# Hybrid attention/convolution encoder layer on one core: TensorE's side matmuls in the middle of their dense tile, and loads and orders changed beside it

## Chip, cores and metric

One core of one Trainium2 chip runs the whole program. The metric is the device time of an execution in microseconds; lower is better. Three executions of the kernel before took 2691.98, 2694.58 and 2695.61 us.

## What is computed

One layer of an encoder, applied to two batches with shared weights: a prompt of 512 tokens and a sample of 2048 tokens, 2560 in all, model width 1024. Inputs and outputs are float32.

```python
h = _rms(x, norm1_g)
proj = h @ w_in                       # 1024 -> 512 q, 128 k, 128 v, 1024 GLU input
q, k = per-head RMSNorm(q), per-head RMSNorm(k)      # 8 query heads, 2 key heads, 64 wide
attn = _window_attention(q, k, v, attn_sink)         # 128-query blocks against 384 keys, ALiBi, sink
u = a * sigmoid(gate); u = depthwise_conv31(u); u = silu(layernorm(u))
x = x + concatenate([attn, u]) @ w_out
h2 = _rms(x, norm2_g)
g = silu(depthwise_conv3(h2 @ ffn_w_gate))           # 1024 -> 2816
x = x + (g * (h2 @ ffn_w_up)) @ ffn_w_down
```

## The kernel before, in words

**Dense work in slots.** Activations lie transposed (features on the 128 partitions, tokens along the row). Each weight tile of 128 outputs is split into a high and a low part (`weights`, float32r), and each activation too (`h_hi`/`h_lo`, `cat_hi`/`cat_lo`, `hw_hi`/`hw_lo`, `mid`); a product is hi*hi + hi*lo + lo*hi. One **slot** is one dense tile: 8 input tiles of 128 times 3 products, 24 matmuls into one bank of PSUM. There are 374 slots (`SLOT`), in phases: A (14 slots for each of 5 chunks of 512 tokens: the input projection, 128x512 results), O (8 slots per chunk: the output projection), and F (66 slots for each of 4 windows of 438 tokens: G, gate and up tiles by turns, then D, down tiles). The order is A0 A1 A2 A3, the first 6 slots of A4, O0, the rest of A4, then F0 with O1 in its middle, F1 with O2, F2 with O3, F3 with O4. The last two windows (406 tokens each) follow in another scheme, 198 block products ("pair" code, from L2250 on), which has no side work.

**Every engine walks the same list of slots.** In its iteration n, ScalarE (ACT) and VectorE (DVE) first handle the result of slot n-1 (`before`): they wait for the counter `s_used` that the last matmul of that tile raises, and evict or post-process it: for a gate tile ACT copies it (`gb`, L1369), DVE applies three taps (`cv`, L1788, L1791, L1794); for an up tile DVE multiplies it in (L1801), ACT and DVE split the product (L1386, L1807). Then they split the weights of slot n+2 (ACT L1144, DVE L1558), then do the side work that the planner's lists `ACT_SIDE[n]` and `DVE_SIDE[n]` name, and DVE ends with a share of the depthwise convolution (`cc`, L1661/L1665), shared out by the room that a planner (`conv_room`) sees in each slot. All queues are strictly in order. So iteration n of ACT and DVE runs beside the dense tile n of TensorE.

**TensorE's side work.** `PE_SIDE[n]` names the small matmuls of slot n: `scores` (6 matmuls, L2208), `transpose` of probabilities (4 per tile, L2219), `values` (8 or 12, L2230), `qk_sum` (L2173), `qk_spread` (L2194), `v_transpose` (L2181), `norm1` (L2156), the LayerNorm and RMSNorm sums (L2238, L2243, L2248). In the kernel before they are issued behind the 24 matmuls of tile n and ahead of tile n+1, each behind its own waits. For attention block N (20 blocks of 128 queries, first slots and steps in `ATTN_AT`) the lists are:

```python
for _t in range(GROUP):                      # GROUP = 4
    PE_SIDE[_b + _t].append(("scores", _N, _t))
    DVE_SIDE[_b + _t + 1].append(("bias", _N, _t))
...
PE_SIDE[_b + 7 + _i // 2].append(("transpose", _N, _g, _k))
ACT_SIDE[_b + 8 + _i // 2].append(("copy_t", _N, _g, _k))
PE_SIDE[_b + 10].append(("values", _N))
```

`scores(N, t)` with t > 0 waits until DVE's `bias(N, t-1)` (L1726, two operations, then small ones) has read the two score banks; that `bias` stands in `DVE_SIDE[b + t]`, the same slot number as the waiting scores. `transpose` number i waits for ACT's copy (`copy_t`, L1289) of transpose i-3; `values` waits for the last copy. `qk_spread(c, m)` waits for DVE's `qk_norm(c, m-1)` (L1629), `norm1` for `token_inverse` (L1565), the sums for DVE's additions of the same slot.

**Loads.** SyncE (SP) issues nearly all loads, in order: in iteration n the weights of slot n+4 (once tile n is done), then what the slot's conditions name. `load_cat(c, half)` loads one half of the output projection's input, a high and a low part: half 0 are the attention rows, half 1 the convolution rows; they were stored from GpSimd's (POOL's) queue (`store_attn`, `store_ln`). Before, half 1 is issued in iteration START["O", c] - 4, half 0 in START["O", c] - 3, and the 8 residual loads in START["O", c] - 1. The first matmul of an O phase waits for all four.

**Start.** The first chunk's norm is applied after the projection: ACT squares `x0` (L1168), DVE adds the squares (L1586, L1589), and TensorE sums them over the partitions (`first_sum`, L2162) behind tile 1. The weights of slots 0 to 3 are split before the loop.

Of the kernel before, what the change touches and what calls it, by code (L numbers as in the profile page):

```python
# [26 lines left out]
KT = D_MODEL // P  # L27
# [60 lines left out]
SLOT = []  # L88
START = {}
# [9 lines left out]
SLOTS = len(SLOT)  # L99
# [75 lines left out]
for _c in range(CHUNKS):  # L175
    _b = AT_SLOT["A", _c, 0]
    if _c + 1 < CHUNKS:
        for _f, _t in ((2, 0), (4, 2)):
            ACT_SIDE[_b + _f] += [("token_squares", _c + 1, _t), ("token_squares", _c + 1, _t + 1)]
        ACT_SIDE[_b + 5].append(("token_root", _c + 1))  # L180
        DVE_SIDE[_b + 5].append(("token_inverse", _c + 1))
        PE_SIDE[_b + 5].append(("norm1", _c + 1))
        ACT_SIDE[_b + 6].append(("scale_copy", _c + 1))
        for _p, _f in enumerate((7, 8, 10, 11)):
            DVE_SIDE[_b + _f].append(("norm_h", _c + 1, _p))
            ACT_SIDE[_b + _f].append(("h_high", _c + 1, _p))
            DVE_SIDE[_b + _f + 1].append(("h_low", _c + 1, _p))
    PE_SIDE[_b + 1 + NORMED].append(("qk_sum", _c))
    PE_SIDE[_b + 7].append(("v_transpose", _c))
    ACT_SIDE[_b + 7].append(("qk_root", _c))  # L190
    ACT_SIDE[_b + 8].append(("v_out", _c))
    DVE_SIDE[_b + 8].append(("qk_inverse", _c))
    ACT_SIDE[_b + 9].append(("qk_high", _c))
    DVE_SIDE[_b + 9].append(("qk_low", _c))
    POOL_SIDE[_b + 9].append(("v_store", _c))
    for _m in range(NORMED):
        PE_SIDE[_b + 10 + _m].append(("qk_spread", _c, _m))
        DVE_SIDE[_b + 11 + _m].append(("qk_norm", _c, _m))
        POOL_SIDE[_b + 12 + _m].append(("qk_store", _c, _m))

for _c in range(CHUNKS):
# [284 lines left out]
def encoder_layer(nc, x, x_tok, w_in, w_out, w_ffn, w_down, w_pass, params, consts, y):  # L486
    with ExitStack() as ctx:
# [305 lines left out]
        def _(sp):  # L793
# [135 lines left out]
            for p in range(1, PIECES):  # L929
                load_first(p)  # L930
            load_weight(1)
            sp.dma_start(pick[:], consts[:, C_PICK:C_SPREAD]).then_inc(s_const, 16)
            sp.dma_start(ident[:], consts[:, P:2 * P]).then_inc(s_const, 16)
            sp.dma_start(spread_raw[:], consts[:, C_SPREAD:C_BIAS]).then_inc(s_const, 16)
            sp.dma_start(bias[:], consts[:, C_BIAS:C_SLOPE]).then_inc(s_const, 16)
            sp.dma_start(slope[:], consts[:, C_SLOPE:C_COLS]).then_inc(s_const, 16)
            load_weight(2)
            load_weight(3)
            u_v = u_d.rearrange("j p n -> p j n")
            edges = (0, PROMPT_U - HALO, PROMPT_U, U_COLS - HALO)  # L940
# [15 lines left out]
            for n in range(SLOTS):  # L956
                s = SLOT[n]
                if n + RING < SLOTS:
                    load_weight(n + RING)
                if EDGES_AT <= n < EDGES_AT + len(edges):  # L960
                    store_edge(n - EDGES_AT)
                if PADS_AT <= n < PADS_AT + len(pads):
                    store_pad(n - PADS_AT)
                if s[0] == "A" and s[1] + 1 < CHUNKS:
                    c, f = s[1] + 1, s[2]
                    if f == 0:
                        load_xt(c, 0)
                        load_xt(c, 1)
                        load_xs(c, 0)
                        load_xs(c, 1)  # L970
                    if f == 2:
                        load_xt(c, 2)
                        load_xt(c, 3)
                    if f in (8, 9):
                        load_xs(c, f - 6)
                if n == START["F", 0, 0] - 4:
                    for p in range(PIECES):
                        load_window(0, p)
                if s[0] == "D" and s[2] == 1 and s[1] + 1 < PLAIN and 1 <= s[3] < 1 + PIECES:
                    load_window(s[1] + 1, s[3] - 1)  # L980
                if s[0] == "G" and s[2] == 0 and s[4] == 1 and 1 <= s[3] < 1 + KT:
                    load_y(s[1], s[3] - 1)
                for c in range(CHUNKS):
                    if n == START["O", c] - 4:
                        load_cat(c, 1)
                    if n == START["O", c] - 3:
                        load_cat(c, 0)
                    if n + 1 == START["O", c]:
                        load_residual(c)
                if n in PAIR_LOADS:  # L990
                    load_pair_window(0, PAIR_LOADS[n])
                if n == LAST + GU_TILES:
                    for a in ("A21", "A22", "A11", "A12"):
                        load_part(0, a)
# [142 lines left out]
        def _(act):  # L1137
# [320 lines left out]
            for p in range(1, PIECES):  # L1458
                first_high(p)
            weight_high(1)  # L1460
            weight_high(2)
            for p in range(PIECES):
                first_squares(p)
            weight_high(3)
            act.wait_ge(s_const, 16 * 5)
            nc.scalar.activation(spread[:], spread_raw[:], ACT.Copy).then_inc(s_sprd, 1)
# [88 lines left out]
        def _(dve):  # L1555
# [367 lines left out]
            for p in range(1, PIECES):  # L1923
                first_low(p)
            weight_low(1)
            weight_low(2)
            for p in range(1, PIECES):
                first_add(p)
            weight_low(3)
            dve.wait_ge(s_const, 16 * 5)  # L1930
            nc.vector.tensor_scalar(qg[:], slope[:, 0:AT], col("q_g"), None, ALU.mult).then_inc(s_set, 1)
# [103 lines left out]
        def _(pe):  # L2035
# [34 lines left out]
            def project(n, c, f):  # L2070
                e = OUTPUT["A", c, f]
                bank_free(e)
                weight_ready(n)
                out = bank[out_bank(e)]
                hi, lo, a, b = h_hi[c % 2], h_lo[c % 2], whi[n % RING], wlo[n % RING]
                for k in range(KT):
                    if f == 0 and k % PK == 0:
                        pe.wait_ge(s_hlo, PIECES * c + k // PK + 1)
                    for i, (l, r) in enumerate(((a, hi), (a, lo), (b, hi))):
                        mm = nc.tensor.matmul(out[:], l[:, k, :], r[:, k, :],  # L2080
                                              start=(k == 0 and i == 0), stop=(k == KT - 1 and i == 2))
                mm.then_inc(s_used, 1)
# [21 lines left out]
            def out_project(n, c, o):  # L2104
                e = OUTPUT["O", c, o]
                bank_free(e)
                weight_ready(n)
                if o == 0:
                    pe.wait_ge(s_cat, 64 * (c + 1))
                out = bank[out_bank(e)]  # L2110
                a, b = whi[n % RING], wlo[n % RING]
                for k in range(KT):
                    for i, (l, r) in enumerate(((a, cat_hi), (a, cat_lo), (b, cat_hi))):
                        mm = nc.tensor.matmul(out[:], l[:, k, :], r[:, k, :],  # L2114
                                              start=(k == 0 and i == 0), stop=(k == KT - 1 and i == 2))
                mm.then_inc(s_used, 1)

            def gate_up(n, w, h, i, s):
                e = OUTPUT["G", w, h, i, s]
                bank_free(e)  # L2120
                weight_ready(n)
                if h == 0 and i == 0 and s == 0:
                    pe.wait_ge(s_hwlo, PIECES * (w + 1))
                a, b = whi[n % RING], wlo[n % RING]
                out = bank[out_bank(e)][:, 0:TC if s else TH]
                for k in range(KT):
                    for j, (l, r) in enumerate(((a, hw_hi), (a, hw_lo), (b, hw_hi))):
                        mm = nc.tensor.matmul(out, l[:, k, :], r[:, k, 1:TC + 1] if s else r[:, k, :],  # L2128
                                              start=(k == 0 and j == 0), stop=(k == KT - 1 and j == 2))
                mm.then_inc(s_used, 1)  # L2130

            def down(n, w, h, i):
                weight_ready(n)
                a, b = whi[n % RING], wlo[n % RING]
                for q in range(KT):
                    o, k = divmod(KT * i + q, FH)
                    e = OUTPUT["D", w, h, o]
                    out = bank[out_bank(e)][:, 0:TC]
# [157 lines left out]
                        mm.then_inc(s_dn, 1)  # L2296
                mm.then_inc(s_used, 1)

            pe.wait_ge(s_set, 4)
            for n in range(SLOTS):  # L2300
                s = SLOT[n]
                if s[0] == "A":
                    c, f = s[1], s[2]
                    if n == 0:
                        first_project()
                    else:
                        project(n, c, f)
                    if n == 1:
                        first_sum()
                        pe.wait_ge(s_const, 16 * 5)  # L2310
                elif s[0] == "O":
                    out_project(n, s[1], s[2])
                elif s[0] == "G":
                    gate_up(n, *s[1:])
                else:
                    down(n, *s[1:])
                for t in PE_SIDE[n]:
                    if t[0] == "norm1":
                        spread_scale(t[1])
# [14 lines left out]
                    elif t[0] == "ln_var":  # L2334
                        ln_var(t[1])
                    elif t[0] == "norm2":
                        norm2_sum(t[1])
            pe.wait_ge(s_y, 2 * KT * PLAIN - 3)
            for k in range(PRODS):
                if PROD[k][0] == "P":  # L2340
# [84 lines left out]
```

## Time and profile before

| | us |
|---|---|
| three executions | 2691.98, 2694.58, 2695.61; median 2694.58 |
| the profiled execution | 2696.35, its span 2694.5 |
| TensorE matmul busy | 2645.7 (98% of the span) |
| TensorE weight load busy | 2346.5 (87%) |
| VectorE busy | 1822.0 (68%) |
| ScalarE busy | 1259.0 (47%) |
| GpSimd busy | 193.6 (7%) |
| mean granted TensorE clock | 0.995 |

The span is from the first to the last instruction of the profiled execution; 1.85 us of its time lie around the span. A matmul's end is modelled, and matmuls overlap in the pipeline, so "98% busy" is not 98% of the peak; the distance between the starts of two matmuls says how fast they go.

### The profile page before, as it was taken

How to read it: one execution, taken by the hardware profiler on the slowest of the kernel's cores; microseconds unless marked ns; L12 is line 12 of the kernel's file. 1: busy time of each engine (PE TensorE's matmuls, PEld its weight loads, DVE VectorE, ACT ScalarE, POOL GpSimd, SP SyncE). 2: the span in 40 equal slices, each digit the busy share in tenths (PEclk: the TensorE clock that was granted, in tenths of full speed). 3: DMA queues.
4: the chain of work that ended last, by engine and by line, in shares of the span. 5: the costliest groups of instructions: out<-in, count | busy, mean ns of one | idle time of the engine just before them, and what ended most of it. 6: DMA issues, size and time to landing. Idle time of an engine off the chain costs nothing.

```text
span 2694.5 us, 35290 instructions
## 1 busy us (share of the span) xinstructions
PE 2645.7 (98%) x13216; PEld 2346.5 (87%) x13216; DVE 1822.0 (68%) x3020; ACT 1259.0 (47%) x2031; POOL 193.6 (7%) x332
## 2 busy tenths in 40 slices
PE   8999999999999999999999999999999999999998
PEld 6777777788888998888998888998889999999998
DVE  4665747798676876576877577877256576766764
ACT  5354564466535447336446336447134333433432
POOL 0110021100010000110000110000010000000001
PEclk9999999999999999999999999999999999999999
DMA  8867769734753443753443753443754522221211
GB/s 319 319 215 250 255 239 364 269 124 130 269 184 118 150 133 112 295 182 114 153 134 114 278 179 125 149 134 125 270 174 159 182 76 62 71 63 59 67 55 66
DMA packets 138761, 453.74 MB, mean 168 GB/s; under 512 B 24448, under 2 KB 37120, under 8 KB 121952
## 3 DMA queue, kind: packets, MB, share of 16 engines
q1 hardware_dynamic: 111616, 349.17, 38.4%
q0 software_dynamic: 26976, 102.32, 10.5%
q8 instruction: 106, 1.74, 0.3%
q14 instruction: 63, 0.52, 0.1%
HBM read 362.63 MB, written 88.79 MB: 168 GB/s over the span
## 4 chain that ended last, share of the span: by engine, by line
PE 90%; DMA 3%; DVE 3%; ACT 2%; issue 2%; SPq 0%; POOL 0%; DVEq 0%; ACTq 0%; POOLq 0%
PE bank L2128 31%; PE bank L2144 14%; PE bank L2276 12%; PE bank L2080 10%; PE bank L2114 8%; PE bank L2292 7%; PE bank L2230 2%; PE bank L2208 2%; PE bank L2219 2%; DMA cat_lo<-cat_scratch 2%; DMA xt<-x_tok 1%; DMA wraw<-w_in_t 0%; PE bank L2194 0%; PE bank L2173 0%; DVE xs L1573 0%
## 5 line engine op out<-in xcount | busy, mean ns | idle before, releaser
L2128 PE MATMUL bank<-hw_hi,weights 128*128 128x440 f32 (+1 forms) x2816 | 812.3, 365 | 0.0
L2128 PEld LDWEIGHTS bank<-hw_hi,weights 128*128 128x128 f32 x2816 | 530.0, 188 | 47.9 <-issue 12.9
L2128 PE MATMUL bank<-hw_lo,weights 128*128 128x440 f32 (+1 forms) x1408 | 510.8, 363 | 0.0
L2144 PE MATMUL bank<-mid,weights 128*128 128x438 f32 x2112 | 431.9, 364 | 0.0
L2144 PEld LDWEIGHTS bank<-mid,weights 128*128 128x128 f32 x2112 | 396.0, 189 | 33.3 <-issue 6.8
L1558 DVE TENSOR_TENSOR weights<-wraw,weights 128x1024 fp32r<-128x1024 f32 x286 | 348.8, 1220 | 106.0 <-ACT weights L1144 105.3
L1665 DVE SCALAR_TENSOR_TENSOR cc<-win,par,cc 128x512 f32<-128x512 f32 x600 | 414.3, 743 | 0.0
L1144 ACT ACTIVATE weights<-wraw 128x1024 fp32r<-128x1024 f32 x286 | 301.7, 1055 | 236.2 <-DMA wraw<-w_down_t 157.1
L2080 PE MATMUL bank<-h_hi,weights 128*128 128x512 f32 x1104 | 360.2, 400 | 0.0
L2128 PEld LDWEIGHTS bank<-hw_lo,weights 128*128 128x128 f32 x1408 | 264.4, 188 | 16.6 <-issue 1.0
L2080 PEld LDWEIGHTS bank<-h_hi,weights 128*128 128x128 f32 x1104 | 209.2, 189 | 53.5 <-issue 5.7
L2080 PE MATMUL bank<-h_lo,weights 128*128 128x512 f32 x552 | 218.2, 395 | 0.0
L2114 PE MATMUL bank<-cat_hi,weights 128*128 128x512 f32 x640 | 204.9, 396 | 10.7 <-DMA cat_lo<-cat_scratch 10.7
L1401 ACT ACTIVATE part_hi<-part_raw 128x512 fp32r<-128x512 f32 x198 | 119.8, 623 | 152.5 <-DMA part_raw<-w_pass_t 88.6
L2292 PE MATMUL bank<-mid,part_hi 128*128 128x406 f32 x704 | 188.2, 348 | 2.3 <-DVE mid L1899 1.9
L1843 DVE TENSOR_TENSOR part_lo<-part_raw,part_hi 128x512 fp32r<-128x512 f32 x198 | 134.7, 687 | 65.7 <-ACT part_hi L1401 63.7
L2114 PEld LDWEIGHTS bank<-cat_hi,weights 128*128 128x128 f32 x640 | 121.7, 190 | 39.8 <-issue 14.4
L1369 ACT ACTIVATE gb<-bank 128x440 f32<-128x440 f32 x88 | 47.2, 536 | 221.8 <-PE bank L2128 217.1
L1788 DVE TENSOR_SCALAR cv<-gb,par 128x438 f32<-128x438 f32 x88 | 44.8, 509 | 147.7 <-ACT gb L1369 147.5
L2292 PEld LDWEIGHTS bank<-mid,part_hi 128*128 128x128 f32 x704 | 131.1, 189 | 4.3 <-DVE mid L1899 4.0
L2114 PE MATMUL bank<-cat_lo,weights 128*128 128x512 f32 x320 | 125.9, 394 | 0.0
L2080 PEld LDWEIGHTS bank<-h_lo,weights 128*128 128x128 f32 x552 | 104.6, 190 | 23.5 <-issue 0.8
(215 smaller groups left out, 3724.3 us busy)
## 6 DMA issues: line engine op xcount, KB each, us to landing
weights<-weight_scratch SPq DMA_DIRECT2D x88, 1024.0 KB, 5.6
wraw<-w_ffn_t SPq DMA_DIRECT2D x176, 512.0 KB, 3.5
wraw<-w_down_t SPq DMA_DIRECT2D x88, 512.0 KB, 3.5
weight_scratch<-weights POOLq DMA_DIRECT2D x22, 1024.0 KB, 7.7
part_raw<-w_ffn_t SPq DMA_DIRECT2D x88, 256.0 KB, 2.7
part_raw<-w_pass_t SPq DMA_DIRECT2D x44, 256.0 KB, 2.6
cat_hi<-cat_scratch SPq DMA_DIRECT2D x10, 1024.0 KB, 7.2
cat_lo<-cat_scratch SPq DMA_DIRECT2D x10, 1024.0 KB, 10.2
```

What stands on the lines that cost most here:

```text
L1144: nc.scalar.activation(whi[n % RING], wraw[n % RING][:], ACT.Copy).then_inc(s_whi, 1)
L1401: nc.scalar.activation(p_hi[k % HI_RING][:], p_raw[part_of(k)][:], ACT.Copy).then_inc(s_whi, 1)
L1558: nc.vector.tensor_tensor(wlo[n % RING], wraw[n % RING][:], whi[n % RING].bitcast(F32), ALU.subtract) \
L1665: nc.vector.scalar_tensor_tensor(acc, win[i][:, tap:tap + TB], w_tap, acc, ALU.mult, ALU.add).then_inc(s_cv, 1)
L1843: nc.vector.tensor_tensor(p_lo[part_of(k)][:], p_raw[part_of(k)][:], p_hi[k % HI_RING][:].bitcast(F32), ALU.subtract).then_inc(s_wlo, 1)
L2080: mm = nc.tensor.matmul(out[:], l[:, k, :], r[:, k, :], start=(k == 0 and i == 0), stop=(k == KT - 1 and i == 2))
L2114: mm = nc.tensor.matmul(out[:], l[:, k, :], r[:, k, :], start=(k == 0 and i == 0), stop=(k == KT - 1 and i == 2))
L2128: mm = nc.tensor.matmul(out, l[:, k, :], r[:, k, 1:TC + 1] if s else r[:, k, :], start=(k == 0 and j == 0), stop=(k == KT - 1 and j == 2))
L2144: mm = nc.tensor.matmul(out, l[:, q, :], mid[:, k, part, :], start=(k == 0 and j == 0), stop=(k == FH - 1 and j == 2))
L2208: mm = nc.tensor.matmul(bank[SCORE[g]][:, P * ks[0]:P * (ks[-1] + 1)], q[rows, t, :], k[rows, P * (n + ks[0]):P * (n + ks[-1] + 1)], start ...
L2276: mm = nc.tensor.matmul(out, l[:, t, :], r[:, t, cols], start=(p in (1, 2, 5) and t == 0 and j == 0), stop=(t == KH - 1 and j == 2), skip_ ...
L2292: mm = nc.tensor.matmul(bank[BANK_Y[n % 4]][:, 0:TP], l[:, (deep * o + t) % KH, :], mid2[:, t, part, i, :], start=(t == 0 and z == 0), sto ...
```

## The change

Of the kernel's text it moves these things; nothing is computed that was not computed before.

1. The side work of slot n is issued by a new helper `side_work(n)`, called inside the loop of `project`, `out_project`, `gate_up` and `down` behind the 12th of the 24 matmuls (k or q == 4 of 8). Slot 0, whose tile is `first_project`, keeps it behind. `first_sum` stays behind tile 1.
2. `h_high` (ACT's split of the next chunk's input) goes one slot later; DVE's `h_low` stays, so that both are in the same slot.
3. `qk_norm` goes to the head of its slot's list on DVE.
4. At the start the load of the weights of slot 2 goes ahead of the five loads of constants; ACT's squares and DVE's additions go ahead of the split of those weights.
5. For chunks 1 to 4 half 0 of `cat` is loaded in iteration START["O", c] - 6 instead of - 3, now ahead of half 1.

```diff
@@ -183,7 +183,7 @@
         for _p, _f in enumerate((7, 8, 10, 11)):
             DVE_SIDE[_b + _f].append(("norm_h", _c + 1, _p))
-            ACT_SIDE[_b + _f].append(("h_high", _c + 1, _p))
+            ACT_SIDE[_b + _f + 1].append(("h_high", _c + 1, _p))
             DVE_SIDE[_b + _f + 1].append(("h_low", _c + 1, _p))
@@ -195,7 +195,7 @@
     for _m in range(NORMED):
         PE_SIDE[_b + 10 + _m].append(("qk_spread", _c, _m))
-        DVE_SIDE[_b + 11 + _m].append(("qk_norm", _c, _m))
+        DVE_SIDE[_b + 11 + _m].insert(0, ("qk_norm", _c, _m))
         POOL_SIDE[_b + 12 + _m].append(("qk_store", _c, _m))
@@ -929,12 +929,12 @@
             load_weight(1)
+            load_weight(2)
             sp.dma_start(pick[:], consts[:, C_PICK:C_SPREAD]).then_inc(s_const, 16)
...
             sp.dma_start(slope[:], consts[:, C_SLOPE:C_COLS]).then_inc(s_const, 16)
-            load_weight(2)
             load_weight(3)
@@ -983,7 +983,7 @@
                     if n == START["O", c] - 4:
                         load_cat(c, 1)
-                    if n == START["O", c] - 3:
+                    if n == START["O", c] - (6 if c else 3):
                         load_cat(c, 0)
@@ -1458,9 +1458,9 @@
             weight_high(1)
-            weight_high(2)
             for p in range(PIECES):
                 first_squares(p)
+            weight_high(2)
             weight_high(3)
@@ -1923,9 +1923,9 @@
             weight_low(1)
-            weight_low(2)
             for p in range(1, PIECES):
                 first_add(p)
+            weight_low(2)
             weight_low(3)
@@ -2074,6 +2074,8 @@
                 for k in range(KT):
+                    if k == KT // 2:
+                        side_work(n)
                     if f == 0 and k % PK == 0:
                         pe.wait_ge(s_hlo, PIECES * c + k // PK + 1)
...
@@ -2296,24 +2304,8 @@
+            def side_work(n):
+
                 for t in PE_SIDE[n]:
                     if t[0] == "norm1":
                         spread_scale(t[1])
...
+            pe.wait_ge(s_set, 4)
+            for n in range(SLOTS):
...
+                else:
+                    down(n, *s[1:])
+                if n == 0:
+                    side_work(n)
```

The same two lines (`side_work(n)` at k or q == KT // 2) stand in `out_project`, `gate_up` and `down`.

## Rows read from the trace of the kernel before

**Rows 1.** The page: the span, and TensorE's busy time.
```profile
span 2694.5 us, 35290 instructions
PE 2645.7 (98%) x13216; PEld 2346.5 (87%) x13216; DVE 1822.0 (68%) x3020; ACT 1259.0 (47%) x2031; POOL 193.6 (7%) x332
```

**Rows 2.** What TensorE waited for, whole run: us in total, times, longest.
```profile
PE bank L2114 <- DMA cat_lo<-cat_scratch: 10.7, 4, 3.4
PE bank L2194 <- DVE qk L1629: 5.4, 3, 4.5
PE bank L2162 <- DVE x_acc L1589: 4.7, 1, 4.7
PE bank L2208 <- DVE row_max L1726: 2.6, 4, 1.1
```

**Rows 3.** The chain of waits, G tiles of slots 272 to 275: start, us, what.
```profile
1619.52 0.73 PE bank L2208 x6
1620.24 5.01 PE bank L2128 x24
1625.25 0.72 PE bank L2208 x5
```

**Rows 4.** The timeline of VectorE beside rows 3: start, us, line and operation.
```profile
1620.13 0.51 DVE L1788 TENSOR_SCALAR cv<-gb,par 128x438 f32<-128x438 f32 x1
1621.97 1.22 DVE L1558 TENSOR_TENSOR weights<-wraw,weights 128x1024 fp32r<-128x1024 f32 x1
...
1623.59 0.55 DVE L1726 CUSTOM_DVE_ANT_0 S<-bank,bias 128x384 f32<-128x384 f32 x1
...
1628.67 0.55 DVE L1726 CUSTOM_DVE_ANT_0 S<-bank,bias 128x384 f32<-128x384 f32 x1
```

**Rows 5.** The chain of waits between D tiles of slots 292 and 293.
```profile
1719.15 0.72 PE bank L2208 x6
```

**Rows 6.** The timeline of VectorE beside rows 5.
```profile
1721.83 0.55 DVE L1726 CUSTOM_DVE_ANT_0 S<-bank,bias 128x384 f32<-128x384 f32 x1
```

**Rows 7.** The chain of waits, transposes behind the G tile of slot 279.
```profile
1651.13 0.87 PE bank L2219 x8
```

**Rows 8.** The timeline of ScalarE beside rows 7.
```profile
1654.26 1.06 ACT L1289 ACTIVATE S<-bank 128x512 f32<-128x512 f32 x2
```

**Rows 9.** The chain of waits, A tiles: slots 16 and 17, then 70 and 71.
```profile
127.13 0.55 PE bank L2208 x6
...
484.51 5.80 PE bank L2080 x24
...
498.66 0.79 PE bank L2208 x6
```

**Rows 10.** The timeline of VectorE in the first of these two stretches.
```profile
128.19 0.42 DVE L1726 CUSTOM_DVE_ANT_0 S<-bank,bias 128x256 f32<-128x256 f32 x1
```

**Rows 11.** Groups by line: xcount, then busy us and mean ns of one.
```profile
L2208 PE MATMUL bank<-kw_hi,qt_hi 64*128 64x384 f32 x128 | 28.4, 440 | 0.8 <-DVE row_max L1726 0.8
...
L2219 PE MATMUL bank<-ident,S 128*128 128x128 f32 x448 | 58.2, 272 | 0.2 <-ACT S L1289 0.2
```

**Rows 12.** The chain of waits: the last `cat` load of chunk 1.
```profile
712.90 11.40 DMA cat_lo<-cat_scratch
```

**Rows 13.** Stretches: us, then per engine busy us (instructions), granted clock, DMA share, GB/s.
```profile
26.90:35.20 8.30, 8.30 (x27) 6.20 (x26) 2.65 (x5) 6.40 (x9) 0.60 (x2) 0.70 1.01 366
...
711.00:724.00 13.00, 11.52 (x62) 10.60 (x60) 8.51 (x14) 4.95 (x10) 0.00 (x0) 1.00 1.01 427
724.00:732.00 8.00, 7.57 (x28) 6.11 (x29) 1.14 (x3) 0.00 (x0) 0.00 (x0) 0.79 1.02 411
1117.00:1128.00 11.00, 9.17 (x46) 8.30 (x44) 5.36 (x11) 4.16 (x8) 0.00 (x0) 1.00 1.01 425
```

**Rows 14.** The timeline of the start: ScalarE's third weight split, VectorE's last addition.
```profile
18.10 1.06 ACT L1144 ACTIVATE weights<-wraw 128x1024 fp32r<-128x1024 f32 x1 [4.71 <-DMA wraw<-w_in_t]
...
25.00 0.69 DVE L1589 TENSOR_TENSOR x_acc<-x_acc 128x512 f32<-128x512 f32 x1
```

More of the change, by code:

```diff
@@ L2112, in out_project @@
                 for k in range(KT):
+                    if k == KT // 2:
+                        side_work(n)
                     for i, (l, r) in enumerate(((a, cat_hi), (a, cat_lo), (b, cat_hi))):
@@ L2126, in gate_up @@
                 for k in range(KT):
+                    if k == KT // 2:
+                        side_work(n)
                     for j, (l, r) in enumerate(((a, hw_hi), (a, hw_lo), (b, hw_hi))):
@@ L2135, in down @@
                 for q in range(KT):
+                    if q == KT // 2:
+                        side_work(n)
                     o, k = divmod(KT * i + q, FH)
@@ L2297, in pair_down @@
                 mm.then_inc(s_used, 1)
[L2299 to L2316, printed above, removed]
+            def side_work(n):
                 for t in PE_SIDE[n]:
@@ L2337, in _ @@
                         norm2_sum(t[1])
+            pe.wait_ge(s_set, 4)
+            for n in range(SLOTS):
+                s = SLOT[n]
+                if s[0] == "A":
+                    c, f = s[1], s[2]
+                    if n == 0:
+                        first_project()
+                    else:
+                        project(n, c, f)
+                    if n == 1:
+                        first_sum()
+                        pe.wait_ge(s_const, 16 * 5)
+                elif s[0] == "O":
+                    out_project(n, s[1], s[2])
+                elif s[0] == "G":
+                    gate_up(n, *s[1:])
+                else:
+                    down(n, *s[1:])
+                if n == 0:
+                    side_work(n)
             pe.wait_ge(s_y, 2 * KT * PLAIN - 3)
```

## The prediction, made before the changed kernel was built or run

> **What bounds the kernel now.** I read the page first: TensorE's matmuls are busy for 2645.7 of 2694.5 us [rows 1]. Little can be gained by waiting less, and whatever makes TensorE wait costs its full time. Then what TensorE waited for: four items that the change touches, 10.7 us for the load of `cat`, 5.4 for `qk_norm`, 4.7 for the first sum of squares and 2.6 for `bias` [rows 2]. That is 23.4 us, the most that the removal of waits alone can give. Third, the chain of waits beside VectorE's timeline in one stretch [rows 3, 4]: it shows how much room the side work has where it stands. Tile 273 (gate) ends at 1619.52, its scores take 0.73, tile 274 runs from 1620.24 to 1625.25, and only then come the next scores. From the end of tile 273 VectorE does three taps, the weight split and the two `bias` operations, back to back, the last until 1623.59 + 0.55 = 1624.14. The scores behind tile 274 want that `bias`, and find it ready 1.1 us before they start. So the whole side chain is hidden, by about a microsecond, behind a full dense tile. The change takes half of that tile away.
>
> **Part 1, side work in mid-tile.** It adds and removes no matmul. TensorE's stream stays in order, so the second half of the tile is queued behind a side matmul that waits, and with it the end of the tile, `s_used`, the evictions of ACT and DVE, and SP's load of the weights of slot n+4. What was hidden behind 24 matmuls must now be ready after 12. Since iteration n of VectorE begins at the end of tile n-1, the price of a wait is: (producer's end minus end of tile n-1) minus half a tile. A plain G tile takes 4.8 us (24 starts 0.20 apart; 5.01 with the turn back from the scores [rows 3]), so the half is 2.4; an A tile takes 5.5, half 2.75.
>
> - Scores with t > 0, 60 of them (20 blocks, 3 each): 24 fall in G slots, 18 in D, 17 in A and 1 in O, by the planner's list. The number of blocks shows in the 128 + 32 first-product matmuls of scores, two for each of 80 scores; rows 11 has the 128. In G after a gate tile: 1624.14 - 1619.52 = 4.62, less 2.40, is 2.2 us late. After an up tile: 1628.67 + 0.55 = 1629.22, minus 1625.25, is 3.97; 1.6 late [rows 3, 4]. With a mean of 1.9, 24 cost **45 us**. The bounds are 1.2 (if ACT's swish, which lags in this stretch, comes up to date) and 2.4.
> - D: the tile ends at 1719.15, `bias` at 1721.83 + 0.55 = 1722.38 [rows 5, 6]: 3.23 less 2.40 is 0.8 late; 18 cost **15**.
> - A and O, 18: in slot 17 the tile before ends at 127.13 and `bias` at 128.19 + 0.42 = 128.61 [rows 9, 10]: 1.5 us against 2.75, nothing. In slot 71 the tile before ends at 484.51 + 5.80 = 490.31, and the scores start at 498.66 [rows 9]: 8.3 less 2.75 is 5.6 late, of which some was waited for already. The ends are 0 and 5; I take 1.0, since most A slots look like the first: **18**.
> - Transposes in G: behind tile 279, which ends at 1651.13, ACT's first copy ends at about 1654.26 + 0.53 = 1654.79 [rows 7, 8]: 3.66 less 2.40 is 1.3 late. 448 transposes make 112 groups [rows 11], two to a tile; 29 of these tiles are G, of which a third (the first of a block) waits for nothing near, and the third of a block comes off with less. 19 at 0.8: **15**. The 8 like ones in A, with a longer ACT list, at 1.5: **12**. `values` in G, 10 at 0.3: **3**.
> - `norm1` (4), the sums over partitions and the first `qk_spread` of a chunk wait for work of their own slot number too. I have no row for each; bounded by 0 and by half a tile (2.75) for some 12 of them, I take **10**.
>
> The sum is 118 us. The turn into side work and back costs 0.2 us per side tile in either place [rows 3]; I take no difference, with bounds of -10 and +10 us for 174 side tiles.
>
> **Part 2 and 3, `h_high` and `qk_norm`.** `h_high` a slot later frees ACT from waiting for `norm_h`; DVE's `h_low` then waits in its stead, behind it the convolution, in the same slot. No time of its own: `h` of the next chunk is due two slots later, and that is its cover; gone, it would cost 1 us or so per chunk. `qk_norm` first in its list can remove up to 5.4 us [rows 2], but the longest of these waits (4.5) lies in the first chunk, where VectorE is late with all it has, and now the spread asks for it half a tile sooner. I take **-2**.
>
> **Part 4, start.** ACT's third weight split starts at 18.10 after a wait of 4.71 for its load, and the squares stand behind it; DVE's last addition is at 25.00 [rows 14]. With squares first they start at about 13.4 and the sum is there before tile 1 ends at 21: the 4.7 us go [rows 2], and with them the fall of the clock that follows, 8.3 us at 0.70 [rows 13], which cost 8.3 * 0.30 = 2.5. Together **-7**. Late next are the weights of slot 2, at about 20.8, as TensorE comes free for them.
>
> **Part 5, `cat`.** Its last load starts at 712.90, when the DMA engines are full (share 1.01, 427 GB/s), and lands 11.40 us later [rows 12, 13]. Two of the four loads, issued three slots (some 15 us) sooner, find the engines free. On SP they pass two weight loads, which are two tiles ahead of need, and wait for attention stores that are issued four slots before, on POOL's queue. All 10.7 us go [rows 2], and two falls of the clock, 8.0 us at 0.79 each [rows 13], or 1.7 each: **-14**. Late next is the convolution half, one slot earlier than the old last half.
>
> **Sum.** 118 - 2 - 7 - 14 = +95. The profiled execution took 2696.35 (span 2694.5 and 1.85 around it), 1.8 above the median; on the median 2694.6 that is 2789.6, say **2789 us**.
>
> **Rivals.**
>
> *The lists of ACT and DVE catch up (half the stalls).* Both engines are idle for a third of the span or more [rows 1]; each stall of TensorE gives them time to work off what they carry over, above all in the A phases. Against it: in rows 4 the chain starts at the tile's end itself. With half of 118 the sum is +36: 2731.
>
> *The clock oscillates.* TensorE's granted clock was at 2.4 GHz while it waited before 1128 (1.00), and fell to 1.2 GHz for a part of the 8 us after 724 (mean 0.79) [rows 13]. Both followed waits of about 3 us; so the new waits, 1 to 5 us each and in some 95 tiles, are near what tips it. If half of them did at 1.7 each, that adds 80: 2870. Against: most of mine are under 2.3 us. The Trainium skill (TensorE: Matmul & The Clock Gate, "A second HAM failure mode: psum-queue depth-cycling") says that frequent short idles between groups of matmuls make the clock swing between its two levels; by that rule this case would be the likelier one. No row here has such a series of short waits, so none bears it out.
>
> *Faster.* If the bias chain does not begin at the end of the tile but was carried over from the iteration before, its end moves forward with the stall, TensorE soon waits for nothing, and the 23 us of parts 2 to 5 are left: 2672. The point is a mean stall under 0.25 us in these 95 tiles; place: VectorE's taps and weight split ahead of `bias`. Against it: the first tap needs the finished gate tile (1620.13, just after 1619.52 [rows 3, 4]), and 3.4 us of operations follow until the second `bias` starts.
>
> *No change:* stalls and gains cancel at about 23 us of stalls; a coincidence.
>
> **How the numbers follow.** Forecast 0.62, lists catch up 0.19, clock 0.12, faster 0.04, no change 0.03. The range goes from 2731 to 2860: the low end is the second case, the high end takes the upper bounds in G and A (24 * 2.4 and 18 * 3 add 48, turns 10) and part of the clock case. No measurement of this kernel can tell less than about 0.2% (5.4 us) from no change. Faster: 0.04; same 0.03; slower 0.93.
>
> **What would show it.** In the profile after: TensorE waits for `row_max` (L1726) some 50 times, 60 to 80 us in all, in place of 4 times and 2.6; waits for ACT's copies (L1289) some 20 times; tiles in G with scores 7.5 us apart in place of 5.7; `cat` and `x_acc` gone from the list of waits; granted clock near 0.99. I am wrong if the scores' waits sum to under 25 us, or if the clock's mean is below 0.97.

## The result, and the profile after

The kernel after takes 2832.04 us (median of 4 executions, 2828.76 to 2838.28); the kernel before, on the same chip, 2693.28. The ratio is 1.0517, with a 95% interval of 1.0497 to 1.0538: 139 us slower. Forecast were 2789 us, with a range of 2731 to 2860. The profiled execution took 2832.09, its span is 2830.3.

The page of the kernel after, for [rows 1]: the span is 135.8 us longer, the count of matmuls is the same, and yet TensorE is busy for 39 us more.

```profile
span 2830.3 us, 35290 instructions
PE 2684.7 (95%) x13216; PEld 2368.6 (84%) x13216; DVE 1819.5 (64%) x3020; ACT 1255.9 (44%) x2031; POOL 193.4 (7%) x332
```

What TensorE of the kernel after waited for, for [rows 2] (us in total, times, longest):

```profile
PE bank L2216 <- DVE row_max L1726: 56.3, 32, 5.6
PE bank L2238 <- ACT S L1289: 12.4, 10, 4.2
PE bank L2227 <- ACT S L1289: 10.3, 7, 3.1
PE bank L2251 <- DVE ln_acc L1690: 10.2, 4, 3.3
PE bank L2246 <- DVE ln_acc L1675: 9.5, 4, 3.5
PE bank L2102 <- ACT weights L1144: 8.2, 1, 8.2
PE bank L2164 <- DVE t_rs L1565: 6.5, 3, 4.5
PE bank L2216 <- DVE qt_lo L1714: 6.2, 4, 2.2
PE bank L2202 <- DVE qk L1629: 4.4, 4, 2.2
```

`cat` and `x_acc`, 15.4 us in [rows 2], are gone. In their stead stand the scores (L2216) behind `bias`, `values` (L2238) and transposes (L2227) behind ACT's copies, the two LayerNorm sums (L2251, L2246) and `norm1` (L2164). The 8.2 us for the first weights (L2102) were there before, with 8.1. All lines of this view add up to 135.1 us; before it was 39.2. So 96 of the 136 us are new idle time.

The same stretch as in [rows 3], in the chain of waits of the kernel after (start, us, what): the second half of gate tile 273 ends at 1731.05, and tile 274 begins.

```profile
1728.44 2.61 PE bank L2134 x12
...
1731.07 0.55 ACT gb L1369
...
1732.90 0.68 DVE cv L1794
1733.57 1.14 DVE weights L1558
1734.71 0.47 DVE S L1726
1735.17 0.01 DVE row_max L1726
1735.18 0.47 DVE S L1726
...
1735.72 0.79 PE bank L2216 x4
1736.51 3.86 PE bank L2134 x12
```

From the end of the tile the chain goes through ACT's copy, three taps, the weight split and two `bias` operations, and back into TensorE 4.67 us later. TensorE itself has only 12 matmuls to do meanwhile. Its timeline gives what was idle there and one tile earlier (in brackets):

```profile
1727.65 0.45 PE L2216 MATMUL bank<-kw_hi,qt_hi 64*128 64x384 f32 x2 [0.98 <-DVE row_max L1726]
...
1735.72 0.44 PE L2216 MATMUL bank<-kw_hi,qt_hi 64*128 64x384 f32 x2 [2.27 <-DVE row_max L1726]
```

The last line of the chain shows the other loss. The 12 matmuls behind the wait take 3.86 us, the 12 before it 2.61. The windows view of these stretches (us, busy us by engine, granted clock, DMA share, GB/s) says why: the clock was full until 1736 and at 0.67 behind it.

```profile
1727.00:1736.00 9.00, 6.08 (x34) 5.20 (x34) 5.96 (x18) 4.88 (x8) 0.00 (x0) 1.00 0.32 116
1736.00:1740.30 4.30, 4.30 (x19) 3.72 (x18) 0.21 (x2) 1.99 (x3) 0.00 (x0) 0.67 0.00 0
```

Over the whole span the mean granted clock is 0.982 (before 0.995). As an estimate, a mean clock c over a span costs (1 - c) * span: 51 us after, 13 before, 38 more. With 96 us of idle time that makes 134 of the 136 us. I call these two sums "waits" and "clock" below.

### The profile page after: what moved, and what is told of

The parts are those of the page before. It is cut to its first block, busy times and chain, and to the rows that moved or that the text cites. A ratio compares the mean times of both kernels' runs of the same rounds, so it can differ in the third digit from the quotient of the medians.

```text
span 2830.3 us, 35290 instructions
## 1 busy us (share of the span) xinstructions
PE 2684.7 (95%) x13216; PEld 2368.6 (84%) x13216; DVE 1819.5 (64%) x3020; ACT 1255.9 (44%) x2031; POOL 193.4 (7%) x332
## 4 chain that ended last, share of the span: by engine, by line
PE 75%; DVE 10%; ACT 5%; DMA 5%; issue 4%; SPq 0%; POOL 0%; DVEq 0%; ACTq 0%; POOLq 0%
PE bank L2134 24%; PE bank L2284 11%; PE bank L2152 11%; PE bank L2082 8%; PE bank L2118 7%; PE bank L2300 7%; DVE weights L1558 2%; PE bank L2238 2%; PE bank L2216 2%; PE bank L2227 2%; DMA wraw<-w_down_t 1%; DMA xt<-x_tok 1%; DVE S L1726 1%; ACT weights L1144 1%; DVE cc L1665 1%
## 5 line engine op out<-in xcount | busy, mean ns | idle before, releaser
L2134 PE MATMUL bank<-hw_hi,weights 128*128 128x440 f32 (+1 forms) x2816 | 824.0, 369 | 0.0
L2134 PEld LDWEIGHTS bank<-hw_hi,weights 128*128 128x128 f32 x2816 | 539.1, 191 | 52.3 <-issue 16.2
L2134 PE MATMUL bank<-hw_lo,weights 128*128 128x440 f32 (+1 forms) x1408 | 516.9, 367 | 0.0
L1801 DVE TENSOR_TENSOR cv<-bank,cv 128x438 f32<-128x438 f32 x88 | 54.0, 613 | 127.9 <-PE bank L2134 103.7
```

## The experiments

Theory: all the loss comes from the missing distance between a producer and the place of its side work, directly as waits and through them as falls of the clock. Rivals: the turn from dense to side matmuls inside an accumulation costs time; the moved orders (`h_high`, `qk_norm`) cost time; the scores only stand in front of another wait.

| kernel | us | ratio, 95% interval | waits | clock (mean) |
|---|---|---|---|---|
| before | 2693 to 2696 | 1 | 39 | 13 (0.995) |
| after | 2832.0 | 1.0517 (1.0497 to 1.0538) | 135 | 51 (0.982) |
| e1 middle alone | 2869.1 | 1.0647 (1.0621 to 1.0673) | 157 | 57 (0.980) |
| e2 parts 2 to 5 alone | 2669.2 | 0.9906 (0.9889 to 0.9922) | 20 | 8 (0.997) |
| e3 behind 18 of 24 | 2730.6 | 1.0142 (1.0122 to 1.0163) | 69 | 16 (0.994) |
| e10 behind 6 of 24 | 2995.0 | 1.1116 (1.1095 to 1.1137) | 249 | 102 (0.966) |
| e4 scores behind the tile | 2752.0 | 1.0214 (1.0190 to 1.0239) | 71 | 25 (0.991) |
| e5 bias a slot earlier | 2755.3 | 1.0228 (1.0202 to 1.0254) | 79 | 28 (0.990) |
| e6 parts 4 and 5 alone | 2676.3 | 0.9939 (0.9924 to 0.9953) | 30 | 11 (0.996) |
| e7 filler | 2826.5 | 1.0501 (1.0483 to 1.0519) | 102 | 34 (0.988) |
| e8 weight split behind bias | 2796.5 | 1.0382 (1.0365 to 1.0399) | 113 | 28 (0.990) |
| e9 all a slot apart | 2686.8 | 0.9965 (0.9951 to 0.9979) | 33 | 8 (0.997) |
| e11 e9, queries and norm too | 2673.6 | 0.9919 (0.9904 to 0.9934) | 24 | 5 (0.998) |
| e12 the kernel of e2 again | 2670.3 | 0.9908 (0.9891 to 0.9924) | 21 | 5 (0.998) |

Waits are the sum of all lines of the view of TensorE's waits, clock is (1 - c) * span with c to three places (so within 1.5 us), both of the profiled execution, in us. That execution is not always a typical one: in e1 and e4 it is 8 and 6 us faster than the median of the second column, in e6 6 us slower.

### e1 and e2: the two halves of the change

e1 is the kernel after with parts 2 to 5 undone. e2 has parts 2 to 5 and this in TensorE's list:

```diff
                 for k in range(KT):
-                    if k == KT // 2:
-                        side_work(n)
...
-                if n == 0:
-                    side_work(n)
+                side_work(n)
```

> Part 1 alone, parts 2 to 5 undone. My theory: the middle of the tile carries the whole loss and the other parts gain about 20 us, so this is the slowest of all, 2832 + 20 = 2852 us, with cat and the first sum of squares back among TensorE's waits. Rival (h_high a slot later and qk_norm ahead cost time too): at or below 2832.

> Parts 2 to 5 alone, the side work behind the tile as before. My theory: 2693 less the 23 us of waits and clock falls, 2672, half-clock time down from 30 us to some 10. Rival (the waits only move to the next thing that is late): 2685 to 2695. Rival (orders cost): above 2695.

The middle alone costs 174 us (2869.1), parts 2 to 5 alone gain 25 (2669.2, forecast 23), and e2 is the fastest kernel of the study. The whole loss lies in part 1; the rival of the costly orders falls. e1 is also the cleanest measure of part 1's waits: 157 us against 39 before are 118 us more, which is the sum forecast for them. The halves do not add up quite: on top of the middle, parts 2 to 5 gain 37, not 25. In e1 `qk_norm` stands among the waits with nearly three times what it has in the kernel after:

```profile
PE bank L2118 <- DMA cat_lo<-cat_scratch: 12.2, 4, 3.9
PE bank L2202 <- DVE qk L1629: 11.9, 8, 4.3
```

In e2 what the parts aimed at is all but gone. The largest wait that is left is the one for the first weights, and next one for the weights of slot 5 (L2080, at 41.67 us): their load started at 21.94 and took 17.25. Slot 2, which the prediction named as late next, started at 21.00 without a wait.

```profile
PE bank L2100 <- ACT weights L1144: 7.6, 1, 7.6
PE bank L2080 <- DVE weights L1558: 3.4, 1, 3.4
...
PE bank L2208 <- DVE row_max L1726: 1.8, 3, 1.1
...
PE bank L2194 <- DVE qk L1629: 0.7, 2, 0.5
```

### e3 and e10: how far into the tile

```diff
-                    if k == KT // 2:
+                    if k == KT - 2:          # e3; in e10: k == 2
                         side_work(n)
```

> The whole change, but the side work behind the 18th matmul of 24. If the loss is what is missing between the producer and half a tile, each wait shrinks by 1.2 us (G, D) or 1.4 (A): of the 56 us of waits for row_max some 15 are left, the clock falls a few times only, 2715 us. If the loss is the turn from dense to side matmuls and back inside an accumulation, nothing changes: 2830.

> The whole change, with the side work behind the 6th matmul of 24. Behind the tile 2669, after 18 matmuls 2731, after 12 2832: the waits are now late by another 1.2 us each, in some 90 tiles, so idle time of 135 us becomes about 235, and with more waits over 3 us half-clock time rises from 105 to some 180 us (38 us lost): 2965. If the lists of ACT and DVE catch up once TensorE waits this much, it levels off: 2880.

Behind 24, 18, 12 and 6 of the 24 matmuls the time is 2669, 2731, 2832 and 2995 us: each quarter costs more than the one before, 61, 101 and 163. The turn into side work and back is the same in the last three, so it is not what costs. The waits for `bias` in e3, and in e10:

```profile
PE bank L2216 <- DVE row_max L1726: 24.0, 16, 4.2
```

```profile
PE bank L2216 <- DVE row_max L1726: 103.7, 43, 7.0
```

With 56.3 us and 32 times between them: each wait grows by the matmuls taken away, more waits turn up, and the clock takes its share (16, 51, 102 us). The timelines of TensorE show it tile by tile. Ahead of the scores in an up tile (behind a gate tile; 11 of them) it stands idle for 1.08 us in e3, 2.28 in the kernel after and 3.48 in e10, in the median: 1.20 more each time, which is what six matmuls 0.20 apart take. Ahead of those in a gate tile (behind an up tile; 13 of them) it is 0, 0.98 and 2.19.

Both expectations were too low, by 16 and 30 us. For e3 I had expected some 15 us of waits for `bias` and 24.0 were left. For e10 the waits came to 249 us instead of 235, since the scores in D tiles, which waited for 2.5 us in all in the kernel after, waited for 14, and the clock lost 51 us more instead of 38. The engines' lists did not catch up.

### e4: the scores stay behind the tile

`side_work` runs twice, in the middle for all but `scores`, behind the tile for `scores`:

```diff
+def IN_MIDDLE(t):
+    return t[0] != "scores"
...
                 for t in PE_SIDE[n]:
+                    if IN_MIDDLE(t) != middle:
+                        continue
```

> The whole change, but the scores stay behind the tile; all other side work is in its middle. If scores are the bulk, as I forecast (78 of 118 us), waits for row_max (56 us) go but for a few, and with them about half of the clock falls: 2755. If the other side work sets the loss and the scores' waits only stood in front of it: above 2800.

2752.0 against an expectation of 2755. Scores carry 80 us of the 163 that lie between e2 and the kernel after, the rest of the side work the other 83, the clock included in both. I had given the scores 78 of 118, and the rest 40, without the clock. In waits alone it is 64 for the scores (135 to 71) and 51 for the rest (71 to 20).

### e5 and e8: change the chain ahead of the scores

e5: `bias` a slot earlier, possible since the scores are now done in mid-tile. e8: in slots with a `bias`, DVE's weight split goes behind it.

```diff
-        DVE_SIDE[_b + _t + 1].append(("bias", _N, _t))
+        DVE_SIDE[_b + _t].append(("bias", _N, _t))
```

```diff
-                if RING <= n + AHEAD < SLOTS and SPLIT[n + AHEAD]:
+                later = any(t[0] == "bias" for t in DVE_SIDE[n])
+                if RING <= n + AHEAD < SLOTS and SPLIT[n + AHEAD] and not later:
                     weight_low(n + AHEAD)
...
+                if RING <= n + AHEAD < SLOTS and SPLIT[n + AHEAD] and later:
+                    weight_low(n + AHEAD)
```

> The whole change, and bias one slot earlier on DVE's list: since scores(N, t) are now done in the middle of tile b + t, bias(N, t) can stand in DVE_SIDE[b + t] and be ready about when that tile ends, half a tile ahead of the next scores. My theory (too little distance between producer and place): the waits for row_max fall from 56 us to under 10, half of the clock falls go, 2755 us, as with the scores behind the tile. If the loss lay in the engines being out of room as such, about 2830.

> The whole change, and in slots with a bias on DVE's list the weight split (1.22 us) stands behind it instead of ahead. If the waits are the chain that I added up from the end of the tile before, each wait of scores in G and D tiles shrinks by up to 1.2 us: row_max 56 us becomes some 30, 2795. If the bias was held by the scores themselves or by ACT: no change, 2830.

e5 takes 2755.3 us, as expected, and as much as e4: giving the scores distance is worth the same whether the scores go back or the `bias` comes forward. In its list of waits `row_max` does not stand at all; ACT's copies, the LayerNorm sums and `norm1` lead as before. e8 takes 2796.5 (expected 2795). Its waits for `bias`:

```profile
PE bank L2219 <- DVE row_max L1726: 39.8, 33, 5.6
```

About the same number of waits, 16.5 us less, and 23 us less of clock: one operation of 1.22 us taken out of the chain is worth 36 us. Where the split simply stood in the chain, in the up tiles, the idle time fell from 2.28 to 1.14 us. In the gate tiles it fell from 0.98 to 0.59 only, since behind an up tile VectorE now stands idle for 0.64 us until ScalarE has its half of the product (`mid`, L1386) ready; the split had covered that wait. In the A tiles, where some slots load split weights, the waits fell from 17.9 to 15.5 us.

### e7: fill the waits instead of removing them

In the 24 gate and up tiles with scores of t > 0, two matmuls of zero weights go onto the open bank ahead of the side work. They add zero to the result.

```diff
                     if k == KT // 2:
+                        if any(t[0] == "scores" and t[2] > 0 for t in PE_SIDE[n]):
+                            for _ in range(2):
+                                nc.tensor.matmul(bank[out_bank(e)][0:CT * HALO, 0:TC if s else TH], zeros[:],
+                                                 (hw_hi[:, 0, 1:TC + 1] if s else hw_hi[:, 0, :]).bitcast(F32),
+                                                 start=False, stop=False)
                         side_work(n)
```

> The whole change, and in the 24 gate and up tiles with scores of t > 0, ahead of the side work, two matmuls of zero weights onto the open bank (they add nothing; some 1.5 us of TensorE time where it waited 2.2 on average). If the falls of the clock cost time of their own beside the idle time, the eight of them in these tiles (some 41 us at half clock, 20 us lost) go for the most part, while the filled waits cost nothing: 2815. If the clock follows the program anyway or its fall costs nothing: 2832 or more.

The groups by line show the added work, 96 records for 48 matmuls, 40 us:

```profile
L2134 PE MATMUL bank<-hw_hi,zeros 128*60 128x440 f32 x52 | 21.9, 544 | 0.0
L2134 PE MATMUL bank<-hw_hi,zeros 128*60 128x438 f32 x44 | 18.5, 543 | 0.0
```

Waits fell by 33 us and the clock's share by 17; 33 + 17 - 40 is 10, and the profiled span is 9 us shorter than that of the kernel after. The medians are 5.5 us apart, with intervals that overlap, so by time alone this run does not decide whether there is a gain. What it shows is that 40 us of extra matmuls cost nothing: 33 went into waits that were there, and the clock, whose mean over all four executions is 0.986 against 0.982, paid for the rest. The expected gain of 17 us (2815) was too high; the fillers, 1.7 us in each tile, were longer than the 1.0 us that TensorE waited in most gate tiles. That the idle time itself brings the clock down is supported by this run and by the counts of the last section; no run changed the one without the other.

### e9, e11 and e12: distance for everything

```diff
-        PE_SIDE[_b + 5].append(("norm1", _c + 1))
+        PE_SIDE[_b + 6].append(("norm1", _c + 1))
-        DVE_SIDE[_b + 11 + _m].insert(0, ("qk_norm", _c, _m))
+        DVE_SIDE[_b + 10 + _m].append(("qk_norm", _c, _m))
-    PE_SIDE[_l + LN_SUM[_c]].append(("ln_sum", _c))
+    PE_SIDE[_l + LN_SUM[_c] + (1 if _c else 0)].append(("ln_sum", _c))
-    PE_SIDE[_l + _at[5]].append(("ln_var", _c))
+    PE_SIDE[_l + _at[5] + 1].append(("ln_var", _c))
-        DVE_SIDE[_b + _t + 1].append(("bias", _N, _t))
+        DVE_SIDE[_b + _t].append(("bias", _N, _t))
-        ACT_SIDE[_b + 8 + _i // 2].append(("copy_t", _N, _g, _k))
+        ACT_SIDE[_b + 7 + _i // 2].append(("copy_t", _N, _g, _k))
```

e11 adds the same for what e9 still waited for: `load_q`, `attn_q_high`, `attn_q_low` a slot earlier (and `load_kv`, `k_high`, `k_low` for chunks 1 to 4), and the RMSNorm sum a slot later on TensorE. e12 is e2's kernel again, beside e11 on one chip.

> The whole change, with every producer and its side work put a slot further apart: bias, the copies of the transposes and qk_norm one slot earlier on DVE's and ACT's lists, norm1, the four later LayerNorm sums and all variance sums one slot later on TensorE's. If the middle of the tile costs nothing in itself and only the distance counts, nearly all new waits go (135 us of idle to 30 or so) and the clock stays up: 2680, close to the 2669 of the side work behind the tile with its lists as they are. If it costs a turn of its own, or DVE and ACT now wait for TensorE in place of the reverse and are late with the evictions: 2720 or more.

> e9 and the rest of its new waits: the keys and queries of a block are loaded and split a slot sooner, and the RMSNorm sum stands a slot later on TensorE. If the middle of the tile only needs distance, idle time falls from 33 us to some 22, and the time to 2673, as with the side work behind the tile. If something else of 10 to 15 us hangs on the middle: 2685, as e9.

> The kernel of e2 once more, beside e11 on one chip, for the comparison of the two: 2669 us again, if e2's time was no chance.

With side work in the middle of every tile e9 takes 2686.8 us and e11 2673.6: the loss of 163 us against e2 has shrunk to 3. e9's largest new wait, before e11 took it away, was:

```profile
PE bank L2216 <- DVE qt_lo L1714: 7.5, 4, 2.2
```

So the middle of the tile costs next to nothing in itself, and it gives nothing either. e12 took 2670.3 us, 3.3 less than e11; all its executions (2669.1 to 2671.3) are below all of e11 (2672.5 to 2674.5), and e11's profile has 3 us more of waits, so the difference is probably real and lies in waits that are left. Scores in neighbouring G tiles follow each other 5.73 us apart in e11 and 5.75 in e2 (medians), so leaving an open tile and coming back costs no more than the same work behind it. e2 stays the version to keep, 0.9% faster than before and the simpler one.

## Why the prediction was right, and what was off

**Direction and mechanism: right.** The price of a wait, (producer's end minus end of the tile before) minus half a tile, was forecast from [rows 3, 4] as 2.2 us behind a gate tile and 1.6 behind an up tile. In the same tiles of the kernel after it is 2.27 (tile 274) and 0.68 (tile 275), and over all G tiles 2.28 and 0.98 in the median. The second is under its lower bound of 1.2, for the reason given there: ACT's swish (L1375), which ended 0.3 us after the up tile 274 before, now ends 3.3 us ahead of that tile's end, at 1737.06. e3, e10 and e8 move the two sides of that difference one at a time, and the idle time in the up tiles follows by 1.1 to 1.2 us a step.

**The sum of waits: right in total, wrong in parts.** Forecast: 118 us added, 23 removed, 95 net. Of the 23, some 6 are falls of the clock, so in waits alone the forecast is 101 net. Measured: 39.2 to 135.1, that is 96 net; part 1 alone adds 118 (e1). The parts are less good (idle time ahead of the scores with t > 0, from TensorE's timeline, and lines of the list above, in us):

| | forecast | kernel after |
|---|---|---|
| scores in G | 45 | 36 |
| scores in D | 15 | 2.5 |
| scores in A and O | 18 | 18 |
| transposes | 27 | 10.3 |
| `values` | 3 | 12.4 |
| `norm1` and the sums | 10 | 10.2 + 9.5 + 6.5 = 26 |
| a block's first scores, behind the split of its queries (`qt_lo`) | none | 6.2 |

Three things were wrong in the reading. In D the chain of [rows 6] does not begin with the end of the tile: its weight split follows convolution operations without a gap, and in the kernel after it starts before the tile's end, so that the scores of slot 293 waited for 0.05 us instead of 0.8. In A the mean of 1.0 us was 11 waits of nothing and 7 of 1.3 to 5.6. And the item for `norm1` and the sums, for which I had no rows, had a bound of half a tile (2.75 us) that does not hold, with single waits of 4.5, 3.5 and 3.3 us. The signs said some 50 waits for `row_max` with 60 to 80 us, and there are 32 with 56; tiles in G with scores 7.5 us apart, and they are 8.3 apart in the mean. That the parts made up for one another is luck.

**The clock: the step that failed.** The sum holds nothing for new falls of the clock; they stood there as a rival with a chance of 0.12 (half of some 95 waits bring one, at 1.7 us each: 80 us, 2870). The profile shows 38 us more lost to it, in 16 more falls (22 stretches at 1.2 GHz against 6 before, by the trace's clock records), nearly all of the 43 us by which 2789 was too low. The result lies between the forecast and that rival. The argument against it, "most of mine are under 2.3 us", was too weak a one: waits of that length are where it begins (counted in the last section). The rule of the Trainium skill (TensorE: Matmul & The Clock Gate, "A second HAM failure mode: psum-queue depth-cycling"), that frequent short idles between groups of matmuls make the clock swing, pointed the right way, and this trace agrees in part: the clock did swing, but the falls went with the length of the single gap (10 of 10 over 3 us, 3 of 41 under 2 us).

**Catch-up: wrong case, as rated.** With TensorE waiting more, ACT's and DVE's lists did not recover: from e3 to e10 the waits grew from 69 to 249 us, and in the up tiles the idle time is the same 2.28 us in 8 of 11. Only the swish did.

**Parts 2 to 5: right.** Forecast -23, measured -25 (e2). Parts 4 and 5 gain 18 (e6, forecast 21), the orders 7 (forecast 2). What is missing from the 21 is at the start: TensorE begins slot 4 8.2 us sooner in e2 than before (32.55 against 40.71), but then waits 3.4 us for the weights of slot 5, so that slot 5 begins 4.6 us sooner (41.67 against 46.28), where 7 were forecast.

> Parts 4 and 5 alone (start and cat loads), all orders and the side work as before. By my terms 21 us of the 25 that parts 2 to 5 gained: 2673. If the orders (h_high, qk_norm) carry half of it: 2682.

e6 took 2676.3. `qk_norm`'s wait is back in it, which is what the orders had taken away:

```profile
PE bank L2194 <- DVE qk L1629: 6.7, 4, 4.5
```

I had expected the first chunk's wait of 4.5 us to stay whatever stands first on DVE's list; with the side work behind the tile it goes.

## What to carry to other kernels

Where side work sits in an in-order stream is a due time: before moving it up, take for each item the end of its producer relative to the event that starts the producer's chain, and compare that with what the engine has left to do until the new place. Moving the work by half a tile cost 163 us here, and moving the producers (or the place) by one slot gave back all but 3, so move both sides together or neither. Check first that the chain does begin with that event: in D tiles it did not, and the forecast there was six times too high. And price a wait of TensorE with the clock that it may take along: here that added some 40% to the idle time.

## What the runs showed of the hardware

Whether TensorE's clock fell went with how long it had just stood idle. Counted over the starts and modelled ends of all matmuls against the clock records, this many gaps were followed by a fall (within 5 us of their end):

| idle gap | before | after | e1 | e10 |
|---|---|---|---|---|
| 0.3 to 2 us | 2 of 13 | 3 of 41 | 4 of 45 | 5 of 65 |
| 2 to 2.5 us | none there | 5 of 13 | 3 of 12 | 7 of 12 |
| 2.5 to 3 us | 0 of 2 | 3 of 4 | 4 of 4 | 12 of 12 |
| over 3 us | 3 of 3 | 10 of 10 | 15 of 16 | 24 of 24 |

While it lasts, a fall costs a little under half of the time: 12 matmuls of a G tile took 4.67 us at 1.2 GHz against 2.61 at 2.4 GHz, the second of these rows from slot 124, the first from slot 123 just ahead of the wait (the chain of waits of the kernel after):

```profile
852.65 2.61 PE bank L2134 x12
...
862.58 4.67 PE bank L2134 x12
```

I had not expected that an open accumulation can be left for another bank and taken up again at practically no cost: with nearly all new waits gone (e11), the kernel with 174 tiles interrupted in their middle takes 3.3 us longer than the one with the same work behind them (e12), 0.02 us a tile.
